# Output projection by pairs of token tiles in seven products, with its weight sums made during the second branch

## The reference

```python
branch_a = jnp.einsum('bte,ed->btd', attn * jax.nn.silu(a_z), w_branch_attn)
...
branch_m = jnp.einsum('bte,ed->btd', h_m, w_branch_mlstm)

merged = jax.nn.sigmoid(g_attn) * branch_a + jax.nn.sigmoid(g_mlstm) * branch_m
return x + jnp.einsum('btd,de->bte', merged, w_out)
...
return rms_norm(x, final_norm_w)
```

## Time and profile before

| | us |
|---|---|
| median of three runs | 1135.27 (1134.72 to 1135.38) |
| the profiled execution | 1134.48 |
| its span, first to last instruction | 1132.7 |
| PE busy in the span | 1110.4 |
| second branch on PE | 950.8 to 1039.0 |
| output projection on PE | 1039.0 to 1126.2 |
| after the last matmul | 6.5 |

### The profile page before, as it was taken

The page is one execution under the profiler, slowest core; times in us unless marked ns, Lnnn a source line. Parts: engine busy times, 40 slices in busy tenths (PEclk is TensorE's granted clock), DMA queues, the critical chain, the costliest instruction groups (busy, mean ns, idle before and its releaser), DMA issues.

```text
span 1132.7 us, 16545 instructions
## 1 busy us (share of the span) xinstructions
PE 1110.4 (98%) x5411; PEld 886.4 (78%) x5411; DVE 737.1 (65%) x1201; ACT 466.4 (41%) x1112; POOL 603.3 (53%) x416
## 2 busy tenths in 40 slices
PE   5999999999999999999999999999999999999997
...
GB/s 227 44 96 87 38 93 93 29 122 64 37 157 39 28 131 38 38 47 86 92 38 39 83 102 37 37 83 97 44 48 361 112 93 161 140 108 74 93 74 93
DMA packets 108513, 99.20 MB, mean 88 GB/s; under 512 B 7164, under 2 KB 93560, under 8 KB 108456
## 3 DMA queue, kind: packets, MB, share of 16 engines
...
## 4 chain that ended last, share of the span: by engine, by line
PE 82%; DVE 8%; ACT 3%; DVEq 3%; issue 2%; ACTq 1%; DMA 0%; SPq 0%
PE ps L928 43%; PE ps L1157 15%; PE ps L841 3%; PE ps L1204 3%; PE ps L1205 3%; PE ps L1209 3%; PE ps L1015 2%; PE ps L1131 1%; PE ps L1115 1%; PE ps L1119 1%; PE ps L1128 1%; DVE v L2190 1%; PE ps L1057 1%; DVE row_max L1960 1%; PE ps L1064 1%
## 5 line engine op out<-in xcount | busy, mean ns | idle before, releaser
L753 POOL TENSOR_TENSOR ring_lo<-w,ring_hi 128x512 fp32r<-128x512 f32 x128 | 179.8, 1423 | 134.6 <-ACT ring_hi L1263 134.5
L753 POOL TENSOR_TENSOR ring_lo<-t,ring_hi 128x512 fp32r<-128x512 f32 x96 | 136.3, 1426 | 142.7 <-ACT ring_hi L1263 142.7
L928 PE MATMUL ps<-s_hi,ring_hi 128*128 128x512 f32 x512 | 203.5, 397 | 0.0
L928 PE MATMUL ps<-s_lo,ring_hi 128*128 128x512 f32 x512 | 202.7, 396 | 0.0
L928 PE MATMUL ps<-s_hi,ring_lo 128*128 128x512 f32 x512 | 202.0, 394 | 0.0
L928 PE MATMUL ps<-h_hi,ring_hi 128*128 128x512 f32 x384 | 151.9, 396 | 0.0
L928 PE MATMUL ps<-h_hi,ring_lo 128*128 128x512 f32 x384 | 151.9, 396 | 0.0
L928 PE MATMUL ps<-h_lo,ring_hi 128*128 128x512 f32 x384 | 151.4, 394 | 0.0
L1263 ACT ACTIVATE ring_hi<-w 128x512 fp32r<-128x512 f32 x128 | 75.7, 620 | 93.7 <-PE ps L928 79.6
L928 PEld LDWEIGHTS ps<-s_hi,ring_hi 128*128 128x128 f32 x512 | 96.2, 188 | 22.2 <-issue 3.1
L928 PEld LDWEIGHTS ps<-s_hi,ring_lo 128*128 128x128 f32 x512 | 96.2, 188 | 21.7 <-issue 2.6
...
## 6 DMA issues: line engine op xcount, KB each, us to landing
w<-in_w_in SPq DMA_DIRECT2D x128, 256.0 KB, 3.0
xs<-in_x SPq DMA_DIRECT2D x8, 512.0 KB, 6.4
ga_scratch<-ev ACTq DMA_DIRECT2D x4, 1024.0 KB, 4.8
u_scratch<-silu_z ACTq DMA_DIRECT2D x8, 512.0 KB, 3.3
gm_scratch<-ev ACTq DMA_DIRECT2D x4, 1024.0 KB, 4.8
w_raw<-in_w_branch_attn SPq DMA_DIRECT2D x8, 512.0 KB, 3.8
u_a_f<-u_scratch SPq DMA_DIRECT2D x4, 1024.0 KB, 7.7
ev<-ga_scratch ACTq DMA_DIRECT2D x8, 512.0 KB, 3.5
```

The lines of the kernel that those rows point to most:

```text
L753: return nc.gpsimd.tensor_tensor(flat(lo[:]), flat(raw_or_sum[:]), flat(hi[:]).bitcast(F32), ALU.subtract)
L928: mm = nc.tensor.matmul(ps[:, bank, :], w[:, k, :], h[:, k, :], start=(m == 0), stop=(m == PRODUCT - 1))
```

## The change

The output projection is done for two token tiles at a time, split once along the contraction (`merged` features 0 to 511 and 512 to 1023) and once along the columns of `w_out`. The four quarter products that each of the two tiles would need, eight in all, are replaced by seven products of sums (Strassen's scheme in Winograd's form, the one the input projection uses). Sums of `merged` are made by POOL (`o_t1` to `o_t4`, four per pair), their high parts by ACT (`o_ring` high), their low parts by POOL (two per pair, three in the first) and DVE (five per pair, four in the first). The sums of `w_out` (`f_s1` to `f_s4`) are made once, by DVE, during the second branch. Seven operands of 2 MB (o11, o12, o22, o_s1 to o_s4) take up 112 KB of each partition, and part of that room is in use by the second branch's own operand until its last tile; so three of the sums are stored to DRAM (`s_scratch`, 1 MB each) and read back at the end of the last tile (`f_again`), and split only then.

The seven products need seven combinations per pair (`half_of`, a PSUM bank by 0.5 plus something, and sums with the residual x), in place of four additions.

The change, cut to what the steps below speak of:

```diff
+        def merged_part(half, o, j):
+
+            n = 2 * o + j
+            return merged[:, KH * half:KH * half + KH, n * P:(n + 1) * P]
...
+            def output_weights():
+                sp.wait_ge(tile_done, BM)
+                for half, dst in ((0, f_o11), (0, f_o21), (1, f_o22), (1, f_o12)):
+                    first = BANK if dst in (f_o21, f_o22) else 0
+                    sp.dma_start(dst[:], wo_rows[:, KH * half:KH * half + KH, first:first + BANK]).then_inc(wo_in, 16)
+
+            def keep_sum(n, made, f):
+                sp.wait_ge(wo_sum, made)
+                sp.dma_start(scr_s[n], f[:]).then_inc(wo_stored, 16)
+
+            for i in range(KT // 2):
                 weights(BM + 2 * i, [(0, wbm_cols, 2 * P * i), (1, wbm_cols, P + 2 * P * i)])
-                if not later(i):
...
-            looped(sp, KT // 2, branch_m_step)
+                if i == 0:
+                    output_weights()
+                    keep_sum(1, 1, f_s1)
+                    keep_sum(0, 2, f_s3)
+                if i == 1:
+                    keep_sum(2, 4, f_s4)
             sp.wait_ge(w_split, BO)
...
+            sp.wait_ge(wo_stored, 16 * 3)
+            for n in range(3):
+                sp.wait_ge(um_free, n + 1)
+                sp.dma_start(f_again[n][:], scr_s[n]).then_inc(wo_again[n], 16)
+            sp.wait_ge(tile_done, BO)
             for j in range(2):
                 sp.dma_start(x_more[:, j, :], x_rows[:, j, :]).then_inc(x_in[j], 16)
...
+            for o in range(OPAIRS):
+                last = o == OPAIRS - 1
                 if not last:
                     for j in range(2):
-                        sp.wait_ge(res_ready, summed[j])
-                        sp.dma_start(x_more[:, j, :], x_rows[:, ds(ahead[j], 1), :].rearrange("p a n -> p (a n)"))\
-                            .then_inc(x_in[j], 16)
+                        sp.wait_ge((c21_out, c12_out)[j], WPAIRS + o + 1)
+                        sp.dma_start(x_more[:, j, :], x_rows[:, 2 * o + j + 2, :]).then_inc(x_in[j], 16)
                 for j in range(2):
-                    sp.wait_ge(y_ready, done[j])
+                    sp.wait_ge(y_ready, 2 * o + j + 1)
                     part = slice(0, BANK) if last and j == 1 else slice(0, D)
-                    sp.dma_start(out_rows[:, ds(rows[j], 1), part].rearrange("p a n -> p (a n)"), ev[:, j, part])\
-                        .then_inc(y_out[j], 16)
+                    sp.dma_start(out_rows[:, 2 * o + j, part], ev[:, j, part]).then_inc(y_out[j], 16)
...
+            for o in range(OPAIRS):
+                i = WPAIRS + o
+                w11_o, w12_o = merged_part(0, o, 0), merged_part(0, o, 1)
+                w21_o, w22_o = merged_part(1, o, 0), merged_part(1, o, 1)
+                pool.wait_ge(merged_ready, KH)
+                if o:
+                    pool.wait_ge(merged_rest, 1)
+                    pool.wait_ge(w5_ready, i)
+                sub(o_t1[:], w12_o, w11_o).then_inc(sum_made, 1)
+                pool.wait_ge(w1_hi, i + 1)
+                sub(o_ring[0][1][:], w11_o, o_ring[0][0][:].bitcast(F32)).then_inc(w1_ready, 1)
+                if o == 0:
+                    pool.wait_ge(merged_ready, KT)
+                pool.drain()
+                sub(o_t2[:], w22_o, o_t1[:]).then_inc(sum_made, 1)
+                pool.wait_ge(w6_hi, i + 1)
+                sub(o_ring[1][1][:], o_t2[:], o_ring[1][0][:].bitcast(F32)).then_inc(w6_ready, 1)
+                if o:
+                    pool.wait_ge(w7_ready, i)
+                else:
+                    pool.wait_ge(tile_done, BO)
+                sub(o_t3[:], w22_o, w12_o).then_inc(sum_made, 1)
+                if o:
+                    pool.wait_ge(w4_ready, i)
+                sub(o_t4[:], w21_o, o_t2[:]).then_inc(sum_made, 1)
+                if o == 0:
+                    pool.wait_ge(w3_hi, i + 1)
+                    sub(o_ring[4][1][:], w22_o, o_ring[4][0][:].bitcast(F32)).then_inc(w3_ready, 1)
...
+                    if freed and b == 1 and term == TERMS - 1 and k in (1, 3, 5):
+                        mm.then_inc(um_free, 1)
...
+            def output_pair(o):
+                i = WPAIRS + o
+                bank_a, bank_b, bank_c, bank_d = O_BANKS[o % 2]
+
+                def output_2():
+                    pe.wait_ge(w2_ready, i + 1)
+                    if o >= 2:
+                        pe.wait_ge(c12_out, i - 1)
+                    terms(bank_c, o_ring[2], o12, 0, PRODUCT).then_inc(p2_done, 1)
...
+                pe.wait_ge(w1_ready, i + 1)
+                if o == 0:
+                    pe.wait_ge(wo_split, 4)
+                if o == 1:
+                    pe.wait_ge(tile_out, BO)
+                if o >= 2:
+                    pe.wait_ge(c21_out, i - 1)
+                terms(bank_a, o_ring[0], o11, 0, PRODUCT).then_inc(p1_done, 1)
+                if o == 0:
+                    output_2()
+                pe.wait_ge(w6_ready, i + 1)
+                if o >= 2:
+                    pe.wait_ge(c22_out, i - 1)
+                terms(bank_b, o_ring[1], o_s2, 0, PRODUCT).then_inc(p6_done, 1)
+                if o:
+                    output_2()
+                pe.wait_ge(w7_ready, i + 1)
+                if o >= 2:
+                    pe.wait_ge(c_out, i - 1)
+                if o == 0:
+                    pe.wait_ge(wo_split, 5)
+                terms(bank_d, o_ring[3], o_s3, 0, PRODUCT).then_inc(p7_done, 1)
+                pe.wait_ge(w4_ready, i + 1)
+                pe.wait_ge(a_copied, i + 1)
+                terms(bank_a, o_ring[0], o22, 0, PRODUCT).then_inc(p4_done, 1)
+                pe.wait_ge(w5_ready, i + 1)
+                pe.wait_ge(b_out, i + 1)
+                if o == 0:
+                    pe.wait_ge(wo_split, 6)
+                terms(bank_b, o_ring[1], o_s1, 0, PRODUCT).then_inc(p5_done, 1)
+                pe.wait_ge(w3_ready, i + 1)
+                pe.wait_ge(c11_out, i + 1)
+                if o == 0:
+                    pe.wait_ge(wo_split, 7)
+                terms(bank_c, o_ring[4], o_s4, 0, PRODUCT).then_inc(p3_done, 1)
+
+            for o in range(OPAIRS):
+                output_pair(o)
...
+            def output_high(n, made, block, f):
+
+                act.wait_ge(wo_sum, made)
+                if n == 3:
+                    act.wait_ge(wo_stored, 16 * 3)
+                A(block[0][:], f[:], ACT.Copy).then_inc(wo_hi_ready, 1)
+
+            for n in range(KT):
+                i, j = divmod(n, 2)
+                if n < 2:
+                    act.wait_ge(tile_out, BM - 1 + n)
+                else:
+                    act.wait_ge(merged_ready, n - 1)
+                gate_row(j, scr_g, n)
+                if n >= 1:
+                    gate_tanh_of((n - 1) % 2, KT // 2 + (n - 1) // 2 + 1)
+                if n == 2:
+                    output_high(0, 3, o11, f_o11)
+                if n == 3:
+                    output_high(1, 4, o12, f_o12)
+                if n == 4:
+                    output_high(2, 4, o22, f_o22)
+                if n == 5:
+                    output_high(3, 4, o_s2, f_s2)
+            gate_tanh_of(1, KT)
...
+            for o in range(OPAIRS):
+                last = o == OPAIRS - 1
+                act.wait_ge(p1_done, WPAIRS + o + 1)
+                if o:
+                    act.wait_ge(y_out[0], 16 * o)
+                A(ev[:, 0, 0:BANK], ps[:, O_BANKS[o % 2][0], :], ACT.Copy, scale=0.5).then_inc(a_copied, 1)
+                if o == 0:
+                    again_high(1, o_s1)
+                    o_high_7(0)
+                o_high_4(o)
+                o_high_5(o)
+                if o == 0:
+                    again_high(2, o_s4)
+                    o_high_3(0)
+                square(o, 0, 0, 0)
+                if not last:
+                    act.wait_ge(merged_rest, 1)
+                    o_high_1(o + 1)
+                square(o, 1, 0, 1)
+                res_root_of(o, 0)
...
+            def output_low(n, block, f):
+                dve.wait_ge(wo_hi_ready, n)
+                V.tensor_tensor(block[1][:], f[:], block[0][:].bitcast(F32), ALU.subtract).then_inc(wo_split, 1)
+
+            for n in range(KT):
+                i, j = divmod(n, 2)
+                last = n == KT - 1
+                if n == 1:
+                    dve.wait_ge(wo_in, 16 * 4)
+                    V.tensor_tensor(f_s1[:], f_o21[:], f_o22[:], ALU.add).then_inc(wo_sum, 1)
+                    dve.drain()
+                    V.tensor_tensor(f_s3[:], f_o11[:], f_o21[:], ALU.subtract).then_inc(wo_sum, 1)
+                if n == 2:
+                    dve.wait_ge(wo_stored, 16 * 2)
+                    V.tensor_tensor(f_s2[:], f_s1[:], f_o11[:], ALU.subtract).then_inc(wo_sum, 1)
+                    dve.drain()
+                    V.tensor_tensor(f_s4[:], f_o12[:], f_s2[:], ALU.subtract).then_inc(wo_sum, 1)
+                if n == 3:
+                    output_low(1, o11, f_o11)
+                if n == 4:
```

(57 more changed lines are left out.)

304 lines of the change are left out of this document (134 added, 170 removed).

## The result

The changed kernel takes 1161.57 us (1160.99 to 1161.73), the kernel before 1135.00 in the same comparison: a ratio of 1.0233, 95% interval 1.0215 to 1.0251. The prediction was 1158 with a range of 1143 to 1166. The profiled execution took 1161.73 us with a span of 1160.0, 27.3 more than the 1132.7 of before.

What follows compares the result with a forecast made beforehand. PE was taken to bound the kernel. On the profiled 1134.5 us, -10.9 + 10.8 + 2.0 + 3.4 + 16.6 + 1.1 = +23.0 gave 1157.5, or 1158 for the median, with a range of 1143 to 1166.

Steps and rivals of the forecast that it cites:

- Matmuls removed: Output projection: 384 matmuls of 512 columns become 336, 48 fewer at 0.227 us on PE's path, -10.9 us.
- Wait for the third tile: Second branch: PE waits for POOL's split of weights loaded behind two stores of sums, 10.8 us, ends 4.7 and 13.5.
- Clock: Behind PE's long wait in the second branch: PE restarts at granted clock 0.50, costing 2.0 us, ends 0 and 2.5.
- Entry: Start of the output projection: PE waits before p2 (1.4) and p7 (2.0), together 3.4 us, ends 1 and 5.
- Rounds: Output projection, p4 of one pair to p4 of the next: DVE's ring outlasts PE's work, 16.6 us, ends 3.5 and 22.
- the exclusion: DVE and POOL: each waits for the other's whole instruction if both read two SBUF operands; inferred for 512 elements.
- third rival: Output stage: stores land later and the clock falls in a wait there too, +4 to +12 us, 1166; chance 0.10.
- The end: End of the kernel: DVE reaches the last combination about 1 us after p3, costing 1.1 us, ends 0 and 2.
- The first rival: Output stage: DVE and POOL overlap, so DVE keeps up; +4.3 us, 1139.6; chance 0.13.
- The second: Second branch: weights overtake the store and new waits stay under the 10.9 us saved; -2.7, 1132.6; chance 0.04.
- The fourth: The stages don't touch: the wait falls on a misread stretch, gains and losses cancel; 1135 us; chance 0.03.
- the signs named: Expected in the profile after: PE's wait of about 11 us at 973, clock 0.50 behind it, p4 to p4 22 us.

Runs made afterwards that it cites:

- weights first: The changed kernel with the third branch tile's weights issued ahead of w_out's loads, the fourth's behind these and ahead of the two sum stores: 1146.31 us, ratio 1.0093.

## Why the prediction was right, step by step

- **Matmuls removed, -10.9.** 10.7 measured in the kernel before.
- **Wait for the third tile, 10.8 against 12.4.** The chain was the one described, each step in its place, with three sizes off. w_out had landed 15.9 us after the branch's start, not 13.9. The rate was as reckoned, 395 GB/s over 11 us; what I had short was the time around it, 2.7 us from the branch's start to the full rate and 2.2 at the end, where I had some 2 us for both. The weights landed 6.9 us after issue, not 6.3. And the split took 6.4, not 7.8: DVE's third sum waited for its store (1.20) and was over before POOL got to its low part, so that DVE cost POOL 2.1 us and not 3.5.
- **Clock, 2.0 against 2.1.** Right in size, but by luck. I took the size from the kernel's start, and both windows that I read there have a granted clock of 1.00, so they don't show the lower pace. What I had wrong besides is when it falls: the earlier trace rows show it at 1.00 for 4 us after the last matmul, which I read as what PE may idle without a loss. It fell at waits of 1.9 to 3.4 us too.
- **Entry, 3.4 against 3.1.** From the stage's start to the first p4 are 14.0 us for 10.9 of work: waits of 1.29 before p2 and 1.22 before p7, and some 0.3 for each restart. The low part for p7 was done 11.1 us after the stage's start, not 11.7.
- **Rounds, 16.6 against 16.7**, 29.0 + 22.1 + 22.7 less three times 19.05. I named the exclusion, the store and DVE's order as the causes, and each has been shown by taking it away. I had the store at 3.3 us as it lay; that SP's order made it so long, I had not seen. What I had not counted is the clock: seven matmuls at p6 of the second pair and eight at p4 of the third ran slow, 3.0 us of PE's time, which the prediction had only in its third rival. They didn't add 3.0, since DVE sets the pace here: with weights first fourteen ran slow at p6, and the round was as long (29.1), with a wait of 1.15 in place of 2.37 before the next p4. A slow p4 does lengthen its round, 22.7 for the 22.0 of weights first. So the clock has some 0.7 of the 16.7, and that the sum is met so closely is luck in part.
- **The end, 1.1 against 1.1.**
- **Outside the change, 2.5**, not predicted: scatter, 0.9 of it before the first matmul, where PE waits for the first inputs.

Sum: 2.5 + 14.6 + 9.1 + 1.1 = 27.3 for the profiled run, where 9.1 is entry and rounds less the 10.9. Of the 4.3 us above the predicted 23.0, 2.5 are outside the change and 1.8 are the branch.

The first rival (DVE and POOL overlap at 512 elements) is refuted by the durations with and without POOL's reads. The second (weights that find their way past the store) didn't come about by itself, though its numbers show what the order was worth. The third came true by half: the clock did fall in waits of the output stage, and the stores landed after 3.7 us for 3.3, but together they didn't bring the 1166. The fourth fell with the 26.6 us. Of the signs named, one was off: DVE's instructions of 512 elements took up to 1.78 us beside POOL, not 1.9 to 2.5.
